# Layer-1 prompt attention of a two-layer decoder step: the compressed branch of 16 heads as one batch, and the first scores ahead of the compression's end

## The reference, cut to what matters

```python
k_cmp = compress_blocks(kv[:, :, 0], cmp_pe[0], cmp_w1[0], cmp_w2[0])   # silu(flat @ w1) @ w2
v_cmp = compress_blocks(kv[:, :, 1], cmp_pe[1], cmp_w1[1], cmp_w2[1])
...
s_c = einsum('bqkgd,bnkd->bqkgn', qg, k_cmp) * scale      # 15 columns per head for the prompt
p_c = masked_softmax(s_c, ok_c)
o_c = einsum('bqkgn,bnkd->bqkgd', p_c, v_cmp)
...
p_s = masked_softmax(s_s, ok_s)                           # selected blocks
p_w = masked_softmax(s_w, ok_w)                           # window
o = g[..., 0:1] * o_c + g[..., 1:2] * o_s + g[..., 2:3] * o_w
```

## Time and profile before

| what | us |
|---|---|
| median of 3 executions | 1375.23 (1372.79 to 1378.37) |
| the profiled execution, its own time | 1367.73 |
| its span in the profile | 1366.1 |
| mean granted TensorE clock over the span | 0.974 |
| the prompt loop, from its first mask addition to the next stage's first matmul | 913.10 to 985.25 |

### The profile page before, as it was taken

One profiled execution on the slowest core, in us unless ns is written; L12 is line 12 of the kernel. 1 busy time (PEld: TensorE's weight loads), 2 busy tenths in 40 slices (PEclk: granted clock), 3 DMA queues, 4 the chain that ended last, 5 costly groups with the idle time before them and its releaser, 6 DMA issues.

```text
span 1366.1 us, 26295 instructions
## 1 busy us (share of the span) xinstructions
PE 1263.1 (92%) x10100; PEld 1017.2 (74%) x10100; DVE 781.4 (57%) x1634; ACT 340.7 (25%) x895; POOL 248.9 (18%) x324
## 2 busy tenths in 40 slices
PE   7997898959997999999999999977789899999998
PEld 4454576746797788799999975555545568999998
DVE  1804646585666572377777528559634317768754
ACT  2124534342332331110000011258643301000000
POOL 0103000054332330211111011052022211112100
PEclk9999799989998999999999999999999999999999
DMA  7437798886535755335444533272056753535351
GB/s 260 144 112 265 250 329 287 276 292 202 196 124 189 244 187 184 123 124 164 145 143 143 178 133 134 69 211 69 1 183 202 234 185 124 183 127 166 128 170 36
DMA packets 151071, 236.12 MB, mean 173 GB/s; under 512 B 10626, under 2 KB 113282, under 8 KB 150530
## 3 DMA queue, kind: packets, MB, share of 16 engines
q1 hardware_dynamic: 138914, 203.09, 44.9%
q0 software_dynamic: 7872, 29.26, 6.3%
q10 hardware_dynamic: 4160, 2.10, 0.6%
HBM read 229.09 MB, written 13.64 MB: 178 GB/s over the span
## 4 chain that ended last, share of the span: by engine, by line
PE 82%; DVE 6%; ACT 4%; DMA 3%; issue 2%; SPq 2%; POOL 0%; POOLq 0%; ACTq 0%; DVEq 0%
PE ps L805 20%; PE ps L588 11%; PE ps L833 11%; PE ps L553 11%; PE ps L899 8%; PE ps L771 5%; PE ps L783 2%; PE ps L695 2%; ACT big L1161 2%; PE ps L1030 2%; PE ps L594 2%; PE ps L747 1%; DMA proj<-in_cmp_w 1%; DMA ring<-in_cache_kv 1%; PE ps L1071 1%
## 5 line engine op out<-in xcount | busy, mean ns | idle before, releaser
L899 PE MATMUL ps<-big,proj 128*128 128x168 f32 (+1 forms) x1024 | 160.7, 310 | 9.6 <-DMA proj<-in_cmp_w 7.8
L553 PE MATMUL ps<-ct,ring 128*128 128x128 f32 x960 | 142.2, 286 | 22.9 <-DMA ring<-in_cache_kv 10.7
L588 PE MATMUL ps<-ring,xT 128*128 128x512 f32 (+1 forms) x384 | 161.7, 577 | 0.7 <-DMA ring<-in_w_in 0.7
L899 PEld LDWEIGHTS ps<-big,proj 128*128 128x128 f32 x1024 | 150.0, 192 | 13.0 <-DMA proj<-in_cmp_w 8.0
L553 PEld LDWEIGHTS ps<-ct,ring 128*128 128x128 f32 x960 | 109.3, 144 | 64.6 <-issue 41.4
L588 PEld LDWEIGHTS ps<-ring,xT 128*128 128x128 f32 x384 | 70.3, 193 | 79.8 <-issue 78.0
L805 PE MATMUL ps<-kT,proj 128*128 128x144 f32 x960 | 124.1, 286 | 0.0
L805 PEld LDWEIGHTS ps<-kT,proj 128*128 128x128 f32 x960 | 120.3, 190 | 0.0
L1161 ACT ACTIVATE big<-ps 128x512 f32<-128x512 f32 (+3 forms) x172 | 87.0, 532 | 103.7 <-PE ps L553 103.0
L2110 POOL TENSOR_TENSOR big<-rows 128x576 f32<-128x576 f32 x22 | 51.0, 2318 | 261.4 <-DVE rows L1740 228.1
L805 PE MATMUL ps<-xT,ring 128*128 128x144 f32 x640 | 84.9, 286 | 0.0
(11 more groups left out here) (296 smaller groups left out, 2081.1 us busy)
## 6 DMA issues: line engine op xcount, KB each, us to landing
ring<-in_cache_kv SPq DMA_DIRECT2D x128, 512.0 KB, 5.8
ring<-in_w_gu SPq DMA_DIRECT2D x44, 1024.0 KB, 7.8
ring<-in_w_in SPq DMA_DIRECT2D x11, 2048.0 KB, 7.9
ring<-in_w_down SPq DMA_DIRECT2D x16, 1408.0 KB, 6.9
ring<-in_cache_kv SPq DMA_DIRECT2D x128, 128.0 KB, 3.5
ring<-in_cache_kv POOLq DMA_DIRECT2D x128, 128.0 KB, 3.3
ring<-in_w_out SPq DMA_DIRECT2D x4, 2048.0 KB, 9.6
ring<-in_state_win SPq DMA_DIRECT2D x16, 512.0 KB, 5.4
```

What stands on the lines that cost most here:

```text
L553: return nc.tensor.transpose(out, in_, C("ident", 0, rows, rows))
L588: last = mm(ps[b + t][:, 0:w], xT[:, k, t * P:(t + 1) * P], src[:, k, :], start=k == 0, stop=k == KD - 1)
L899: last = mm(cmp_out(u, si, n), w1s(s, o)[:, hf * P:(hf + 1) * P], XS[(4 * kp + si) % XB][:, o, 0:n], start=o == 0, stop=o == 7)
```

## The change

1. Chunk 5 (the 48 gate columns) is projected ahead of chunk 4; the gates' sigmoid moves into `project_in`. The load of the compression's first weights comes behind both chunks in the plan.
2. `compress_prompt` starts `products(0)` right behind chunk 4 and splits `products(1)` around the turnings 9 and 10. The scores of the first pair (now without the 15 compressed columns) follow `products(1)`, ahead of the second layer of the compression.
3. The compressed branch leaves the loop. All 16 heads' compressed scores are 32 small products into one PSUM bank (`compressed_scores`, 16 of the even heads, then 16 of the odd), one masked softmax on DVE and ACT in two parts (`shift_compressed`, `weigh_compressed`), and 8 turnings of 128 x 128 in two halves (`turn_compressed`). `values` reads the turned weights of a head from `XC`, at one of four row positions, for which POOL copies `vcp` three times (`m_v`).
4. A head now has two mask additions instead of three, two maxima, four exponentials, six turnings and two copies; the turned weights have four buffers instead of two.

```diff
-PCMP_BANKS = (0, 1)
+PCMP_BANKS = (0, 5)
...
-        IN_ORDER = ([1, 3, 0, 2, 4, 5], [0, 1, 2, 3, 4, 5])
+        IN_ORDER = ([1, 3, 0, 2, 4, 5], [0, 1, 2, 3, 5, 4])
...
-            if i == 5:
-                plan.append((("w1", 0), p_h, 1))
             plan.append((("in", 1, n), in_p[1], 3 * (i + 1)))
+        plan.append((("w1", 0), p_h, 1))
...
                 pe.wait_ge(t_e[1], 8)
-                products(0)
-                turn_qk(1, (8, 9, 10))
+                products(0, 0, 16)
+                pe.wait_ge(in_e[1], 3 * len(nin[1]))
+                turn_qk(1, (8,))
                 turn_hidden(0)
-                products(1)
+                products(1, 0, 4)
+                turn_qk(1, (9,))
+                products(1, 4, 12)
+                turn_qk(1, (10,))
+                products(1, 12, 16)
                 pe.wait_ge(t_e[1], 11)
+                prompt_scores(0)
+                turn_hidden(1)
...
+                def compressed_scores():
+
+                    pe.wait_ge(p_we, 1)
+                    for e in range(2):
+                        if e == 1:
+                            pe.wait_ge(m_s, 1)
+                        for j in range(NH // 2):
+                            for t in range(2):
+                                h = 2 * j + e
+                                a = (h // 4 * 2 + t) * 4 * NCP + h % 4 * NCP
+                                last = mm(ps[6][:, a:a + NCP], qT[64 * e:64 * e + 64, j, t * P:(t + 1) * P],
+                                          kcp[64 * e:64 * e + 64, j // 2, :], start=True, stop=True)
+                        last.then_inc(m_s, 1)
...
-                scores(0)
+                prompt_scores(1)
+                compressed_scores()
                 for j in range(NH // 2 + 1):
-                    if j + 1 < NH // 2:
-                        scores(j + 1)
-                    if j >= 1:
+                    if 1 <= j and j + 1 < NH // 2:
+                        prompt_scores(j + 1)
+                    if j >= 2:
                         values(j - 1)
+                    if j == 2:
+                        turn_compressed(1)
                     if j < NH // 2:
                         turn_w(2 * j)
                         turn_w(2 * j + 1)
+                    if j == 1:
+                        turn_compressed(0)
+                        values(0)
...
                 first(0)
+                keep_prompt_compression()
                 for h in range(NH):
                     if h + 1 < NH:
                         first(h + 1)
                     second(h)
+                    if h == 0:
+                        shift_compressed()
+                    if h == 1:
+                        weigh_compressed()
...
-                    if h >= 1:
+                    if h >= 4:
                         keep_out(h - 1)
+                    if h == 4:
+                        keep_compressed(1)
                     keep(h)
+                    if h == 3:
+                        keep_compressed(0)
+                        keep_out(1)
```

More of the change, by code:

```diff
@@ L929, in compress_prompt @@
                         mm(ps[5][dh * 64:dh * 64 + 64, 0:NW], w2[:, 0, hf, :], hidp[:, hf, 0:NW], start=hf == 0, stop=hf == 1)
-                turn_hidden(1)
                 pe.wait_ge(p_he, 4)
@@ L964, in turn_w, with turn_compressed @@
                         for j in range(3):
-                            turn(ps[4 + br][:, j * P:(j + 1) * P], W[:, br * 384 + j * P:br * 384 + (j + 1) * P])
-                    for t in range(2):
-                        last = turn(ps[6][0:NCP, t * P:(t + 1) * P], W[:, 768 + t * NCP:768 + (t + 1) * NCP])
+                            last = turn(ps[4 + br][:, j * P:(j + 1) * P], W[:, br * 384 + j * P:br * 384 + (j + 1) * P])
                     last.then_inc(a_t[1], 1)
+                def compressed_scores():
+                    pe.wait_ge(p_we, 1)
+                    for e in range(2):
+                        if e == 1:
[7 more added lines that the diff above has]
+                        last.then_inc(m_s, 1)
+                def turn_compressed(half):
+                    if half:
+                        pe.wait_ge(m_k, 1)
+                    else:
+                        pe.wait_ge(m_w, 1)
+                    for j in range(4):
+                        last = turn(ps[6][:, j * P:(j + 1) * P], R[:, 3, (4 * half + j) * P:(4 * half + j + 1) * P])
+                    last.then_inc(m_t, 1)
                 def values(j):
@@ L974, in values @@
                     kv = j // 2
+                    pe.wait_ge(m_v, 3)
+                    pe.wait_ge(m_k, 1 if j < 4 else 2)
                     o = [ps[7][64 * e:64 * e + 64, 0:TP] for e in range(2)]
-                    X = [PTp[:, e, :] for e in range(2)]
+                    X = [PTp[:, (2 * j + e) % 4, :] for e in range(2)]
                     for e in range(2):
-                        mm(o[e], vcp[0:NCP, kv * HD:(kv + 1) * HD], X[e][0:NCP, 768:1024], start=True, stop=False)
+                        r = 32 * ((2 * j + e) % 4)
+                        mm(o[e], vcp[r:r + NCP, kv * HD:(kv + 1) * HD], XC[r:r + NCP, kv * 256:(kv + 1) * 256], start=True, stop=False)
                     for br in range(2):
@@ L1204, in project_in @@
                     roots(i)
+                    if (l, n) == (1, 5):
+                        act.wait_ge(in_e[1], 15)
+                        for t in range(3):
+                            last = f(gates[0:WT[t], t, :], proj[0:WT[t], t, N1 - 48:N1], ACT.Sigmoid)
+                        last.then_inc(g_s, 1)
             def keep_qk(l, which):
@@ L1452, in _ @@
             project_in(1)
-            act.wait_ge(in_e[1], 18)
-            for t in range(3):
-                last = f(gates[0:WT[t], t, :], proj[0:WT[t], t, N1 - 48:N1], ACT.Sigmoid)
-            last.then_inc(g_s, 1)
             for k in range(2):
@@ L2174, in _ @@
             last.then_inc(qb_d[1], 1)
+            pool.wait_ge(p_we, 1)
+            pool.wait_ge(qb_d[1], 1)
+            for j in range(1, 4):
+                nc.gpsimd.tensor_copy(vcp[32 * j:32 * j + NCP, :], vcp[0:NCP, :]).then_inc(m_v, 1)
+                pool.wait_ge(m_v, j)
             for name, _, _ in slim:
```

114 lines of the change are left out of this document (69 added, 45 removed).

## The result

The changed kernel took 1380.99 us in the median (1372.28 to 1389.2), the kernel before, beside it on the same chip, 1372.95 us. The ratio is 1.006, with a 95% interval of 1.0045 to 1.0075: slower by 0.6%, 8.0 us. The forecast was +1.4 us with a range of -7.7 to +10.3 around the median of before, so the range held and its middle was off by 6.6 us. That is just beyond the half percent that I called no change, and I had given a slowdown of that size 0.17; the wide range held, the choice within it was not the likely one.

What follows compares the result with a forecast made beforehand. It took VectorE (7.64 us a pair of heads) and the chain of waits (7.66 us) as equal bounds of layer 1's loop; the terms summed to +1.4 us on the 1375.23 us median, 1376.6 us, range 1367.5 to 1385.5.

Steps and rivals of the forecast that it cites:

- The start, -6.2: Layer 1 up to VectorE's first head: reordered chunks and earlier first scores move its start from 913.10 to 906.9, -6.2 us.
- The compression's end, +0.9: VectorE after the first head's part: waits 0.3 us for the compression, then 0.6 us of copies formerly ahead of the loop.
- The batch, +6.8: VectorE idles before shift_compressed while TensorE runs 64 compressed matmuls in single file, 7.5 us at 0.118 each: +6.8 us.
- a third of it at low clock, +2.0: TensorE's batch: +5.8 us if all 64 matmuls run at 1.2 GHz; a fall within it, a third taken, +2.0 us.
- Work on VectorE, -4.1 and +3.7: VectorE's loop: a head falls from 3.82 to 3.54 us, -4.1; added operations on 480 compressed elements cost +3.7 us.
- Refill, +4.3 less 2.0: Seventh and eighth heads: VectorE idles 3.3 and 1.0 us behind TensorE's queue; its former loop idle of 2.0 us goes.
- The end, -4.0: From VectorE's last head to the next stage: 14.3 us becomes 10.3 with some low clock, -4.0 us.
- the low clock takes over: Rival: 1.2 GHz holds through the batch and returns in each pair, together +7.8 us, 1384.4 us; chance 0.18.
- the batch was not cheap: Denies the rival that the batch takes 3.2 us as in the loop, without a clock fall: 1370.3 us, chance 0.14.
- the first scores were early: Denies the rival that ScalarE's copies and loads end 1.4 us later, delaying first scores: 1378 to 1379 us, chance 0.05.
- whole durations freed: Rival on VectorE's loop: each dropped operation frees its full 0.18 us, 8.6 us instead of 4.1: 1372.1 us, chance 0.07.
- The DRAIN rule: On VectorE: the next operation cannot issue until the pipe is empty; by it the sum is 4.5 us better.

Runs made afterwards that it cites:

- e4_order: Kernel before with only the new chunk order, later sigmoid and turnings 9 and 10 between pieces of products(1); compressed branch stays in each head: ratio 0.9973.
- e1_side: Changed kernel with the 64 compressed matmuls alternating even and odd heads into two banks, mask added in four additions instead of two: ratio 1.0017.
- e12_fill: e11_early plus unread TensorE products: eight around the batch and refill, two ahead of each later pair's turnings, two in the last pair: ratio 0.9929.
- e3_later: Changed kernel with VectorE's shift and weighing of the compressed scores, and ScalarE's exponential for them, one head later: ratio 1.0015.
- e7_ahead: Changed kernel with the fourth pair's scores on TensorE ahead of the turning of the compressed weights and values(0): ratio 1.0043.
- e2_double: Changed kernel with its 64 compressed matmuls computed twice, each half once more into the same columns: ratio 1.018, median 1395.64 us.
- e8_nostall: Changed kernel with the edits of e1_side, e3_later and e7_ahead, and ScalarE's copy of the first output behind the next head's exponentials: ratio 0.997.
- e11_early: e8_nostall with the compressed weights turned earlier, where TensorE had waited for VectorE, and ScalarE copying each half earlier: ratio 0.9964.
- e10_warm: Changed kernel with unread 256-column float32 products added on TensorE at its waits, from the second pair's scores to values(7): ratio 1.021.
- e13_tail: Changed kernel with unread products in the later loop only: two ahead of each pair's turnings from the fourth on, two in the last pair: ratio 1.004.
- e15_late: e11_early plus one unread TensorE product ahead of each later pair's turnings, none in the last pair or around batch and refill: ratio 0.9962.

## Why the prediction was right, and where it failed

The four runs with an edit undone or moved bear out the prediction's mechanism: the start is a gain, the batch is a wait, the refill is another. By its terms, in the profiled pair:

- **The start, -6.2.** Measured 112.0 to 106.3 us, -5.7; TensorE waited 0.2 us more before turning 8 than I had said, and the rest went by in 0.3 more. Right. The order alone, in e4_order's trace, is 1.8 us of it; that leaves 3.9 for the early scores, which no run tried by themselves.
- **The compression's end, +0.9.** VectorE's copy started at 910.43 with no idle before it and cost 0.46 us. Too high by 0.4, since VectorE did not wait for it.
- **The batch, +6.8, and a third of it at low clock, +2.0.** Measured 8.67 us. Together right to 0.2 in this trace, and the choice between the two prices was right: single file, 0.113 a matmul. The other, 3.2 us for 64 side by side, was measured as 3.94 in e1_side and 3.64 in e12_fill. The low clock took 24 of the 64, a third as I had said, at 0.09 us more for each.
- **Work on VectorE, -4.1 and +3.7.** A head takes 3.52 us, forecast 3.54. The added operations took 2.02 (923.15 to 925.17) and 1.89 us (928.77 to 930.66), 3.9. Right, though 15 x 0.18 and 14 x 0.11 are 4.2 and not 4.1; whole durations are not freed, or a head would be 3.3.
- **Refill, +4.3 less 2.0.** Measured 5.06 and 0.43 us at other heads (the wait of 1.0 at the eighth head hardly came), 0.34 in the loop: 5.8. Too small by 1.5. `values(0)` and the turnings ahead of it ran at 1.2 GHz, the first taking 3.80 us (941.35 to 945.15) where the next pair's values took 2.03 (946.78 to 948.81); I had counted 2.1, and 0.9 for all of the clock. That is the likely reason.
- **The end, -4.0.** Measured -3.7 in this trace (14.3 to 10.6). That is luck in part: of the seven traces with this same end (the changed kernel, e1, e3, e7, e2, e8 and e11) it is the only one whose clock stayed up. Five took 15.2 us at a mean clock of 0.56, more than before, and e11_early 13.0.

From the first head to the last that is +13.3 against +11.6, and the stage +3.9 against +1.4. The measured terms make some 12.7 of the 13.3; the rest is in waits too short to be named in a row.

**The step that failed is the clock.** I treated the low clock as a third of one batch (+2.0) and left the end at nearly full clock ("10.3 with some low clock"). Both prices depend on where the clock falls. The same batch took 9.75 us in the changed kernel, 10.98 in e3_later, 11.00 in e7_ahead, 11.52 in e10_warm and 13.90 in e13_tail. The same end took 10.6 us in the changed kernel and 15.2 in e1_side, e3_later and e7_ahead, none of which touches it. The trace I am comparing is the changed kernel's fastest execution, with both at or near their best: its granted clock over the span was 0.968, and the slower ones were at 0.953 to 0.965. A batch of 13.9 and an end of 15.2 would add 8.7 us to its 1372.3, 1381.0, which is near the median. That is an addition of rows from several traces, no measurement of those executions; what is shown is that the prices occur.

It can't be the whole account either. The kernel before has a profiled execution 5.2 us under its median of 1372.95 too, so only 3.5 of the 8.7 us belong to the change. And the stretch ahead of layer 1's projection, in which TensorE has the same instructions in every kernel here, ends anywhere between 798.33 us (e15_late) and 804.53 (e3_later):

```profile
798.33 7.89 PE L592 MATMUL ps<-ring,xT 128*128 128x512 f32 x18
```
```profile
804.53 1.88 PE L592 MATMUL ps<-ring,xT 128*128 128x512 f32 x4
```

Of the 8.0 us between the medians the profiled pair shows 4.5, of which 3.9 arise in the stage; that the clock in the batch and at the end makes the other 3.5 is likely, not shown.

So the rival "the low clock takes over" had about the size (+7.8 on top of my sum is +9.2, measured +8.0), and the wrong place. It asked for slow values in each pair of the steady loop, and the loop ran at 1.00 but for one stretch of 3.4 us. The low clock sits in the batch, in the refill and behind the last head. In the text I weighed the Trainium skill ("TensorE: Matmul & The Clock Gate", Part 4: PE-mode transpose), by which turnings don't count as busy, and concluded no fall that the old loop would not have had. For the loop the trace agrees, but for 3.4 us; for the end, with scores gone from the mix, it does not: before, 3.5 us of it were at 1.2 GHz, and in five of these traces most of it was.

The other rivals fell: the batch was not cheap, the first scores were early (908.25), and a head of 3.52 us leaves no room for whole durations freed. The DRAIN rule that I had weighed for that one (the Trainium skill, "VectorE: DVE Perf Modes", The DRAIN you can't avoid) would give 3.3 us a head by my estimate, and the trace does not agree; the section itself lets an operation that is not held start earlier, which I had left out.

That the batch should go side by side is a thing the profile of before already showed, 8 compressed matmuls in 0.40 us, and the trace of e1_side bears it out. The Trainium skill says the same ("TensorE: Matmul & The Clock Gate", Part 3: Packing small matmuls, The mechanism): matmuls whose operands lie in different row groups run at the same time. For the single file it has the price too (same page, LDWEIGHTS (loading the stationary operand)): the load goes by its columns, by its formula 107 ns for 128; the changed kernel's trace has 113 ns a matmul at full clock. At 1.2 GHz its trace and e13_tail's have 205 and 217, for which that section has no figure.

**What stays open:** how often an execution meets each of the clock's cases, since only profiled ones show their stretches; what makes the stretch ahead of the projection vary by 6.2 us; and why the clock fell in the middle of the dense batch of 913.36 to 923.11 while TensorE idled for a fifth of the loop from 945.5 to 965.8 (16.06 us busy of 20.30) without a fall.

## What to carry to other kernels

- Work pulled out of a loop into one batch gets a wait of its own unless the engine behind it has something else queued: put the consumer a step later (in e8_nostall, where the batch was side by side too, no gap was left), and count the batch at the price of its order (0.057 us a matmul with the halves of the array alternating, 0.113 in single file, 0.217 in single file at 1.2 GHz).
- When one engine's queue is reordered, look at the next engine's queue for what now waits on the work that was put back. e7_ahead won little until ScalarE's copy moved too.
- A single profile of a kernel whose TensorE is lightly loaded is one draw. If a stretch has stood at 1.2 GHz once, price the stretch at both levels, and take the range from that. Products that nobody reads, in waits that are there anyway, may be worth 4 us (e11_early to e12_fill, with intervals that just overlap), but they must be measured first: mine were four times as long as I thought, and in e13_tail and e15_late the clock fell in spite of them.

## What the runs showed of the hardware that I had not expected

- TensorE with hardly an idle moment can run at 1.2 GHz: 24.38 us busy of 24.44 at a mean clock of 0.57 (e2_double), and 13.84 of 13.90 at 0.50 (e13_tail), with matmuls of 15 columns and weight loads of 128.
- The price of that is not a factor on the matmul alone: 64 small matmuls in single file take 7.2 us (an estimate from 42 in 4.74) and took 13.90 us at the two levels, side by side 3.64 and 6.85. Weight loads slow down with it: 41 kept their part of TensorE busy for 4.58 us in the changed kernel's first window of the batch, 23 for 4.80 in the second.
- The lower level came in stretches that lasted beyond the work that went with it: in e13_tail from 913.1 to 953.8, over turnings, scores and values.
